# The first modulation units of a one-core decoder trunk: ten units of w_ada in five pairs, scale ahead of shift, and two input tiles from scaled activations with the shift added as a row

## The reference, cut to what matters

```python
c_act = jax.nn.silu(c)
mod = c_act @ ada_w[l] + ada_b[l]                 # (1024) @ (1024, 6144)
sh1, sc1, g1, sh2, sc2, g2 = jnp.split(mod, 6, axis=-1)
h = rms_norm(x, mix_norm[l]) * (1 + sc1) + sh1
xb, yb = jnp.split(h @ w_in, 2, axis=-1)          # (256, 1024) @ (1024, 2048)
# xb: causal conv of 4 taps, then r and i gates (8 blocks of 128x128), then a scan over the tokens
y = (hs * gelu(yb)) @ w_out
x = x + (1 + g1) * y
```

## Time and profile before

| | us |
|---|---|
| median of 3 runs | 1334.57 |
| lowest and highest | 1333.50, 1335.28 |
| span of the profiled execution | 1330.8 |
| the profiled execution's own whole-program time | not given |
| TensorE busy in the span | 1294.8 |
| VectorE busy | 577.2 |
| ScalarE busy | 267.4 |

### The profile page before, as it was taken

One profiled execution on the slowest core, in us unless ns is written; L12 is line 12 of the kernel. 1 busy time (PEld: TensorE's weight loads), 2 busy tenths in 40 slices (PEclk: granted clock), 3 DMA queues, 4 the chain that ended last, 5 costly groups with the idle time before them and its releaser, 6 DMA issues.

```text
span 1330.8 us, 27861 instructions
## 1 busy us (share of the span) xinstructions
PE 1294.8 (97%) x12266; PEld 810.1 (61%) x12267; DVE 577.2 (43%) x932; ACT 267.4 (20%) x496; POOL 13.0 (1%) x42
## 2 busy tenths in 40 slices
PE   7999899999998999999999999999999999999986
PEld 3888799999844763366345366456545355636622
DVE  2695998888766541232214033132122230422331
ACT  3572444444345540001001001000100000100000
POOL 1000000000000011000000000000000000000000
PEclk9999999999999999999999999999999999999999
DMA  9999758898954269999999999999999999999994
GB/s 353 353 385 338 239 203 310 319 316 312 388 214 162 90 254 399 380 357 418 418 418 418 419 419 419 418 418 418 418 418 418 418 418 419 418 419 418 419 418 198
DMA packets 129436, 477.62 MB, mean 359 GB/s; under 512 B 9408, under 2 KB 36256, under 8 KB 129312
## 3 DMA queue, kind: packets, MB, share of 16 engines
q1 hardware_dynamic: 129008, 475.23, 90.9%
q10 hardware_dynamic: 304, 0.57, 0.1%
HBM read 474.72 MB, written 1.05 MB: 357 GB/s over the span
## 4 chain that ended last, share of the span: by engine, by line
PE 90%; DMA 3%; SPq 3%; ACT 1%; DVE 1%; issue 1%; POOL 0%; ACTq 0%; POOLq 0%; DVEq 0%
PE psum L2077 36%; PE psum L2097 16%; PE psum L1816 5%; PE psum L1817 5%; PE psum L1818 5%; PE psum L1732 4%; SPq L667 3%; PE psum L1881 2%; PE psum L1938 2%; PE psum L1770 2%; PE psum L2055 2%; PE psum L2063 2%; DMA ring<-in_m_w_down 2%; DMA ring<-in_m_w_gu 2%; PE psum L1625 1%; PE psum L1632 1%
## 5 line engine op out<-in xcount | busy, mean ns | idle before, releaser
L2077 PE MATMUL psum<-ring,xe 128*32 128x448 f32 x4704 | 451.5, 539 | 1.4 <-DMA ring<-in_m_w_gu 1.4
L2077 PEld LDWEIGHTS psum<-ring,xe 128*32 128x32 f32 x4704 | 190.2, 110 | 252.0 <-issue 246.6
L2097 PE MATMUL psum<-ring,hT 128*32 128x256 f32 (+1 forms) x3180 | 247.6, 460 | 5.9 <-DMA ring<-in_m_w_down 5.7
L2097 PEld LDWEIGHTS psum<-ring,hT 128*32 128x32 f32 x3180 | 151.0, 110 | 95.8 <-issue 27.2
L1478 DVE TENSOR_TENSOR hs<-sg,psum 128x1344 f32<-128x1344 f32 x10 | 15.5, 1554 | 313.3 <-PE psum L2077 313.3
L1816 PE MATMUL psum<-fh,dhi 128*128 128x256 f32 x384 | 109.9, 286 | 3.7 <-DVE fl L1285 2.5
L1493 DVE STREAM_TRANSPOSE hT<-hs 32x448 f32<-32x448 f32 x120 | 111.8, 943 | 1.6
L1817 PE MATMUL psum<-fl,dhi 128*128 128x256 f32 x384 | 108.7, 283 | 0.0
L1818 PE MATMUL psum<-fh,dlo 128*128 128x256 f32 x384 | 108.6, 283 | 0.0
L864 ACT ACTIVATE dhi<-ring 128x1024 fp32r<-128x1024 f32 x72 | 75.9, 1060 | 90.9 <-PE psum L1818 86.1
L1251 DVE TENSOR_TENSOR dlo<-ring,dhi 128x1024 fp32r<-128x1024 f32 x72 | 88.2, 1225 | 6.9 <-ACT dhi L864 4.7
(11 more groups left out here) (298 smaller groups left out, 1196.3 us busy)
## 6 DMA issues: line engine op xcount, KB each, us to landing
ring<-in_m_w_gu SPq DMA_DIRECT2D x224, 896.0 KB, 23.2
ring<-in_m_w_down SPq DMA_DIRECT2D x118, 896.0 KB, 23.5
ring<-in_ada_w SPq DMA_DIRECT2D x24, 2048.0 KB, 16.1
ring_more<-in_m_w_gu SPq DMA_DIRECT2D x32, 896.0 KB, 22.6
ring<-in_f_w_gu SPq DMA_DIRECT2D x24, 1024.0 KB, 14.3
ring<-in_f_w_down SPq DMA_DIRECT2D x6, 2048.0 KB, 14.7
ring_more<-in_m_w_down SPq DMA_DIRECT2D x10, 896.0 KB, 24.5
ring<-in_a_w_in SPq DMA_DIRECT2D x4, 2048.0 KB, 19.5
```

What stands on the lines that cost most here:

```text
L2077: ins = mm(banks[TB * g:TB * g + TB, seg, 0:SEG], block(n), w[:, c0:c0 + SEG], start=first, stop=last, skip_group_check=True)
L2097: ins = mm(y_banks[TB * g:TB * g + TB, o0 + 256 * part:o0 + 256 * part + size], hT[:, t % 2, i, TB * b:TB * b + TB], raw(at // SW)[:, at % ...
```

## The change

The ten first units of w_ada become ten units of another cut: pair q holds units 2q and 2q+1, and its half h chunks 4h to 4h+3, so that a unit is 4 chunks of 128x1024 in pieces of 4 KB. Pair 1 (the scale) comes first, then w_in's first unit, then pair 0 (the shift). VectorE makes G = A * aff as soon as aff is there. TensorE makes tiles 0 and 1 of xb from G, and adds what the shift contributes: the shift, in a padded form (spad), times w_in's first unit gives a row, which a product with ones adds to every token. H is made by VectorE, and tiles 2 and 3 use it. VectorE's sums of units 4 to 9 become sums of pairs, 128x1024 per operation. gates(2) and gates(3) stand behind mix_in(3), ada(4) and ada(5) behind side_in(0). TensorE and ScalarE wait at the start for 7 constants, and TensorE for the rest behind the statistics. ScalarE's order behind the modulation (L827 on) is as before.

```diff
+        spad = dup[:, 32 * KC:64 * KC].rearrange("p (k m) -> p k m", k=KC)
+        pair_acc = lambda q: (sqb if q % 2 == 0 else qw)[:, :, :].rearrange("p b n -> p (b n)")
+        shift_row = rtmp[:, :]
...
+        ADA_ORDER = (2, 3, 0, 1)
...
+        def pair_unit(q, h):
+
+            src = ada_w[0].rearrange("(k p) n -> p k n", p=P)[:, 4 * h:4 * h + 4, 2 * UC * q:2 * UC * (q + 1)]
+            used = (row_mm, 2 * (1 - q) + h + 1) if q < 2 else (pair_half, pair_done(q) - 1 + h)
+            unit(("pair", q, h), [(lambda s: s[:, :].rearrange("p (k n) -> p k n", k=4), src)], used)
...
-        for v in range(4):
-            ada_unit(v)
+        pair_unit(1, 0)
+        pair_unit(1, 1)
         in_unit(0)
-        ada_unit(4)
+        pair_unit(0, 0)
+        pair_unit(0, 1)
         in_unit(1)
+        pair_unit(2, 0)
         unit("gates", [
...
-        ada_unit(5)
-        ada_unit(6)
+        pair_unit(2, 1)
         in_unit(2)
-        ada_unit(7)
-        ada_unit(8)
+        pair_unit(3, 0)
         in_unit(3)
-        ada_unit(9)
+        pair_unit(3, 1)
+        pair_unit(4, 0)
+        pair_unit(4, 1)
         out_unit(0)
...
+        CONSTS = 16 + SORTED
+        CONSTS_FIRST = 7
...
-            act.wait_ge(consts, CONSTS)
+            act.wait_ge(consts, CONSTS_FIRST)
...
             norm(0, [])
+            row_out(2)
+            row_out(3)
+            then(nc.scalar.activation(lru[:, 0, :], cols[:, CB_LAM:CB_LAM + 8], ACT.Abs), la)
+            then(nc.scalar.activation(lru[:, 1, :], lru[:, 0, :], ACT.Exp, scale=-1.0), la)
+            act.wait_ge(lam_d, 1)
+            then(nc.scalar.activation(lru[:, 3, :], lru[:, 2, :], ACT.Ln), la)
             row_out(0)
             row_out(1)
...
-            for k in range(KC):
-                act.wait_ge(xn_done, k // 2 + 1)
-                act.wait_ge(mod_ready, 1)
-                then(nc.scalar.activation(H[:, k, :], A[:, k, :], ACT.Identity, scale=aff[:, k:k + 1],
-                                          bias=mod[:, k:k + 1]), h_sig)
+            act.wait_ge(shift_mm_in, 1)
+            nc.scalar.activation(shift_row, bank[5][:, :], ACT.Copy).then_inc(shift_row_done, 1)
...
+            for v in (2, 3):
+                ada(v)
+            for k in range(KC):
+                v_.tensor_scalar(G[:, k, :], A[:, k, :], aff[:, k:k + 1], None, ALU.mult).then_inc(scaled_done, 1)
             dve.wait_ge(lam_a, 2)
             then(v_.tensor_scalar(lru[:, 2, :], lru[:, 1, :], 1.0, None, ALU.add), ld)
-            for v in range(ADA_ROWS):
+            for v in (0, 1):
                 ada(v)
+            v_.tensor_copy(spad[:, :, 0], mod[:, 0:KC]).then_inc(shift_ready, 1)
+            for k in range(KC):
+                v_.tensor_scalar(H[:, k, :], A[:, k, :], aff[:, k:k + 1], mod[:, k:k + 1],
+                                 ALU.mult, ALU.add).then_inc(shifted_done, 1)
...
-            ada_chunks(4)
+            pair_chunks(2, 0)
...
             for k in range(4):
                 conv(k)
-            ada(4)
-            ada_chunks(5)
-            for k in range(4, 6):
+            pair_chunks(2, 1)
+            for k in range(4, KC):
                 conv(k)
-            ada_chunks(6)
-            for k in range(6, KC):
-                conv(k)
-            ada(5)
...
+            ada(4)
+            ada(5)
+            pair_chunks(3, 0)
...
-            pe.wait_ge(consts, CONSTS)
+            pe.wait_ge(consts, CONSTS_FIRST)
...
+            def pair_as_rows(q, h):
+
+                w = arrived(("pair", q, h))[:, :].rearrange("p (k n) -> p k n", k=4)
+                for c in range(2):
+                    for k in range(4):
+                        last = mm(row_bank(c)[32 * k:32 * k + 32, :], cpad[:, 4 * h + k, :],
+                                  w[:, k, UC * c:UC * (c + 1)], start=h == 0, stop=h == 1)
                 last.then_inc(row_mm, 1)
...
             stats(0)
+            pe.wait_ge(consts, CONSTS)
             pe.wait_ge(cact_ready, 2)
+            pair_as_rows(1, 0)
             keep_clock(bank[5][:, :], 4)
+            pair_as_rows(1, 1)
             keep_clock(bank[5][:, :], 4)
             ada(2)
             ada(3)
             keep_clock(bank[5][:, :], 4)
...
+            def add_shift(T):
+
+                pe.wait_ge(shift_row_done, 1)
+                for a in range(2):
+                    i = 2 * T + a
+                    last = mm(side_bank(T)[:, SEQ * a:SEQ * a + SEQ], shift_row[:, i * P:(i + 1) * P],
+                              ones[:, None, :].to_broadcast([P, 2, P]), start=False, stop=a == 1, skip_group_check=True)
+                last.then_inc(xb_full, 1)
...
-            mix_in(0)
-            mix_in(1)
+            scaled_in(0)
+            pair_as_rows(0, 0)
+            scaled_in(1, [0])
+            pair_as_rows(0, 1)
+            scaled_in(1, [1])
+            ada(0)
+            ada(1)
+            keep_clock(bank[4][:, :], 4)
+            shift_as_row()
+            mix_in(2, [0])
+            add_shift(0)
+            add_shift(1)
+            mix_in(2, [1])
             for k in range(2):
                 gates(k)
-            ada(4)
-            mix_in(2)
-            for k in range(2, 4):
+            mix_in(3)
+            for k in range(2, 6):
                 gates(k)
-            mix_in(3)
-            for k in range(4, 6):
-                gates(k)
-            ada(5)
             side_in(0, [0])
             for k in range(6, KC):
                 gates(k)
             side_in(0, [1])
+            ada(4)
+            ada(5)
             side_in(1)
-            ada(6)
             side_in(2)
             side_in(3)
...
```

More of the change, by code:

```diff
@@ L263, in build @@
         lru_var = sem("lru_var")
+        pair_half = sem("pair_half")
+        scaled_done = sem("scaled_done")
+        shift_ready = sem("shift_ready")
+        shifted_done = sem("shifted_done")
+        shift_mm_in = sem("shift_mm_in")
+        shift_row_done = sem("shift_row_done")
         lru_beta = sem("lru_beta")
@@ L708, in _ @@
             do(nc.gpsimd.memset(cpad[:, :, :], 0.0))
+            do(nc.gpsimd.memset(spad[:, :, :], 0.0))
             do(nc.gpsimd.affine_select(out=ident[:, :], in_=ones[:, :], compare_op=ALU.is_equal, fill=0.0, base=0,
@@ L1123, in ada_chunk, with pair_chunks @@
                                                  op0=ALU.mult, op1=ALU.add), asum if k == KC - 1 else None)
+            def pair_chunks(q, h):
+                slot, at = full_at[name_of[("pair", q, h)]]
+                dve.wait_ge(ring_full[slot], at)
+                if h == 0:
+                    dve.wait_ge(ada_mm, max(2 * q - 2, ADA_ROWS))
+                for k in range(4 * h, 4 * h + 4):
+                    w = ring[slot][:, 2 * UC * (k % 4):2 * UC * (k % 4 + 1)]
+                    if k == 0:
+                        then(v_.tensor_scalar(pair_acc(q), w, cact[:, 0:1], None, ALU.mult))
+                    else:
+                        then(v_.scalar_tensor_tensor(out=pair_acc(q), in0=w, scalar=cact[:, k:k + 1], in1=pair_acc(q),
+                                                     op0=ALU.mult, op1=ALU.add), ph if k % 4 == 3 else None)
             def ada(v):
-                dve.wait_ge(ada_mm, v + 1)
+                dve.wait_ge(ada_mm, ada_place(v) + 1)
                 total = ada_bank(v)[:, 0:4]
@@ L1671, in stats @@
                     last.then_inc(stat_mm, 1)
[L1673 to L1678, removed]
+            def pair_as_rows(q, h):
[4 more added lines that the diff above has]
+                                  w[:, k, UC * c:UC * (c + 1)], start=h == 0, stop=h == 1)
                 last.then_inc(row_mm, 1)
             def ada(v):
-                if v >= 2:
-                    pe.wait_ge(ada_done, v - 1)
+                at = ada_place(v)
+                if at >= 2:
+                    pe.wait_ge(ada_done, at - 1)
                 if v < ADA_ROWS:
-                    pe.wait_ge(row_done, v + 1)
+                    pe.wait_ge(row_done, at + 1)
                 else:
-                    pe.wait_ge(ada_sum, ada_sum_at(v))
+                    pe.wait_ge(pair_half, pair_done(v // 2))
                 for i in range(UC // P):
@@ L1731, in in_products, with scaled_in, shift_as_row, mix_in @@
                 i = 2 * (T % 2) + a
[L1732 to L1740, removed]
-                    for k in range(KC):
-                        pe.wait_ge(h_done, k + 1)
-                        for a in range(2):
-                            last = in_products(T, k, a, start=k == 0 and a == 0, stop=k == KC - 1, skip_group_check=True)
-                last.then_inc(xb_full, 1)
+                return mm(side_bank(T % 4)[:, SEQ * a:SEQ * a + SEQ], w[:, k, i * P:(i + 1) * P],
+                          (G if T < 2 else H)[:, k, :], **how)
+            def scaled_in(T, halves=range(2)):
+                for k in range(KC):
+                    if T == 0:
+                        pe.wait_ge(scaled_done, k + 1)
+                    for a in halves:
```

(21 more changed lines are left out.)

48 lines of the change are left out of this document (15 added, 33 removed).

## The result

| us | before | changed |
|---|---|---|
| median of 4 runs each | 1334.92 | 1342.99 |
| lowest, highest | 1333.50, 1336.38 | 1341.09, 1347.73 |
| span of the profiled execution | 1330.8 | 1345.9 |
| its own whole-program time | not given | 1347.73 |
| dense stage starts | 142.25 | 150.51 |

The ratio is 1.0066, with an interval of 1.0045 to 1.0088: slower by 8.1 us, where 6.2 was forecast; 1342.99 lies within the range given. The profiled execution is the longest of the four, by 4.4 to 6.6 us.

The account below looks back on a forecast made before the run. It took TensorE's unbroken queue as the bound up to the dense stage. Front -1.3, gates 0 and 1 +0.9, gates 6 and 7 +7.1, start -1.3, clock +0.8 gave +6.2, 1340.8 us; range 1335.8 to 1344.3.

Parts of the forecast that it names:

- Gates 6 and 7: TensorE at gates(6) waits for ScalarE's chain from gates(2): 6.4 us, about 5 in one piece; gates(7) +0.7; together +7.1.
- Front: Statistics' end (T) to first input product: 11.2 us saved, 9.9 put behind the first product; together -1.3.
- Gates 0 and 1: TensorE waits 0.4 and 0.7 us for conv(0) and conv(1) behind VectorE's sums, 0.24 waited before: +0.9.
- Start: Waiting for 7 constants instead of 22 brings T earlier by at most 1.8 us; -1.3 taken.
- the possible 1.8: Most that T could come earlier at the start, bounded by unit two's landing at 17.8 to 18.3.
- Clock: Granted clock falls in the new 5 us gap ahead of gates(6): 0 to 1.6 us, +0.8 taken.
- the end of 0: Lower end of the clock term: the gap at gates(6) passes unpunished, costing 0.
- rival 1: Stall at gates(6) with the clock dropped in full, T not earlier: +8.3, 1342.9 us; chance 0.22.
- I count one for one: Later stages pass on any shift of the dense stage's start unchanged.
- The table load: ScalarE's two loads between gates: 1.28 us each; the skill's drain, 2.8 longer stall for two, not counted.

Follow-up runs that it names:

- e1: Changed kernel with ScalarE's first_tap(3) and gate_acts(4) to (7) directly behind gate_acts(3), all decays behind them: 1334.13 us, ratio 0.9989 against before.
- e3: Changed kernel with gates(2) and gates(3) ahead of mix_in(3) again on TensorE: 1336.32 us, ratio 1.0009 against before.
- e6: Kernel before with one move alone, gates(2) and gates(3) behind mix_in(3): 1342.38 us, ratio 1.0048 against before.
- e2: Changed kernel with 20 fillers in TensorE's gap ahead of gates(6): 1343.25 us, ratio 1.0051 against before.
- e5: Changed kernel with each pair unit loaded by two transfers in pieces of 2 KB: 1342.48 us, one run.
- e7: Changed kernel with e1's ScalarE order, gates in pairs between half tiles, second half of VectorE's pair 3 sum behind the scan: 1334.54 us, ratio 1.0002 against before.
- e9: e7 with 16 fillers instead of 5 at the start and 22 instead of 12 ahead of the dense stage: 1336.69 us, ratio 1.0005 against before.
- e10: e9 with 14 fillers at two attention waits, ada(8) and (9) behind the last round's second output product, VectorE's ada(8) later: 1331.33 us, ratio 0.9967 against before.
- e12: Changed kernel with all fillers (start, ahead of the dense stage, attention), its order untouched: 1341.46 us, ratio 1.0044 against before.
- e4: Changed kernel with TensorE and ScalarE waiting for all constants at the start again: 1342.88 us, one run.
- e8: Kernel before with e1's ScalarE order: 1335.34 us, ratio 1.0000 against before.
- e11: Kernel before with the fillers in attention and the 22 ahead of the dense stage: 1333.84 us, ratio 0.9984 against before.

## Why the prediction was right

**Gates 6 and 7, the main term: right in place, cause and size.** gates(6) started gates(2)+13.63, where the prediction had 13.4. Against the 6.93 of work between them it stood 6.70 (6.4 predicted), of which 4.95 in one piece ("about 5"). gates(7) followed 0.7 later than the work alone. That is 7.4 for 7.1. e1, e3 and e6 show the cause.

**Front: right in sum.** The first scaled product came at T+8.38 (T+8.4 predicted). From T to gates(0), with mix_in(2) added to before's side since it moved ahead, took 39.69 against 33.71+6.91: -0.9, where the prediction had -1.3. Gates 0 and 1 waited 0.69 (gates(1) alone), 0.5 more than before, for +0.9 predicted. Together -0.4, as predicted. The sums at 1285 ns and H at 407 ns were as taken; G, at 348 ns, was quicker than its 0.41.

**Start: mis-sized, and its 0.8 is a lucky draw.** "No row gives their landing", and most of the possible 1.8 was taken. The parameters landed late, at 8.5, so the first transpose came only 0.84 earlier (8.48 for 9.32). T followed it by 7.5 in both kernels and so moved by 0.8, not 1.3. The slow transposes of x, 3.49, cost nothing here: ScalarE's squares let the statistics start 3.8 to 3.9 behind the first transpose in both. In the other five profiled runs with this start (e1, e2, e3, e5, e7) the statistics products took 3.97 to 4.79 instead of 3.72, and T was 16.11 to 17.33. The mean of the six, 16.50, is 0.3 earlier than before's 16.77, and e5 is 0.6 later. The 16 fillers mend it: T is 15.51, 15.50 and 15.72 in e9, e10 and e12, and the statistics take 3.72 in all three.

**Clock: mis-sized, and one place missed.** The step took +0.8, the middle of 0 to 1.6. The records say 1.9: gates(6) and gates(7) took 0.3 and 0.85 more than their work and wait, and the half tile 4.23 instead of 3.47 to the next start, 0.76. e2 says 1.84 by another way. The same gap of 4.94 to 4.95 cost less elsewhere, by the same reading 1.0 in e4, 0.9 in e5 and 1.35 in e12, where the clock came back sooner. It never cost nothing; the end of 0 was no real one. The Trainium skill, "TensorE: Matmul & The Clock Gate", "HAM oscillation — how this bites in real kernels", which lets an array kept waiting start its next work cold, has this right for the gap at the gates.

**Sum at the dense stage:** T -0.8, front and gates 0 and 1 -0.4, gates 6 and 7 +7.4, clock +1.9: +8.1, and 8.26 was measured. The prediction's +6.2 lacks 0.5 at the start, 0.3 at the gates and 1.1 of clock. The measured 1342.99 is nearer to rival 1's 1342.9 than to the forecast's 1340.8: the same stall, the clock dropped in full, T not earlier. The first of these two conditions held, and with 0.3 in the mean the second nearly did.

**"I count one for one" failed by its clock.** The dense stage passed its start on with 1.5 us more, since the clock fell once more. The same stood in e1, e2, e4, e5 and e6 (229.8 to 229.9 from dense to K/V), not in before, e3, e7, e8, e9, e10, e11 and e12 (228.4). The median does not have all of it, as before's own runs from 1333.1 to 1341.2 may well have such falls.

**The table load.** Both switches in this stretch of the changed kernel read as the one of before does: 1.28 at 69.61 with the next activation at 70.90, and 1.28 at 76.04 with the next at 77.33. The Trainium skill, "ScalarE: Activation LUTs", "What ACT_TABLE_LOAD costs", adds a drain of 1.38 us to each. By it gates(6) would have come 2.8 later; it came 0.2 later than forecast (13.63 for 13.4), so the trace does not agree.

**What the change is worth without the loss.** e3 has T 0.7 and the front 0.9 earlier, yet its dense start is 1.24 later than before's. Four of its gates start 0.65 to 0.70 late, since conv and gate_acts come 1.55 us apart and a gate takes 0.86. What was won in the front is given back at the gates. Between e10 and e11, which share the fillers of the dense and attention stages, lie 2.5 us (the intervals of the ratios just overlap). This is the change together with a fitting order of three engines and a start without gaps; how it divides among these was not tried.

## What to carry to other kernels

When a piece of work moves in one engine's queue, lay the partner's queue beside it and take the distance from its feeder to the work that its result frees. Here ScalarE needed 13.4 us from gates(2) on, TensorE had 14.7 us of other work before the change and 7.0 after it. The price here was the wait and the half-rate work behind it. Filling the gap recovered the second part only (e2), reordering recovered both (e1, e3).

## What was not expected of the hardware

**The same short waits lower the clock in some executions and not in others.** The 2.47 us before the dense stage passed at 1.00 in the profiled run of before and fell to 0.52 in that of after. Two waits of 1.8 and 1.6 us in attention did the same, and so did the wait of 1.30 in e7. These falls are worth 1.5, 3.0 and 1.3 us. The first two would explain why the kernel before spreads over 6.8 us on one chip. With fillers at the dense start and in attention the highest of e11's 12 runs was 1336.37 and the highest of e10's 1332.92, while 11 of 30 runs of before on that chip lay above 1337. That the fillers narrow the spread is not shown by this: e12, which has them, spreads over 5.0 us in 7 runs, and e1, which has none of them, over 4.0 in 12 (1332.50 to 1336.47). What decides whether a wait is punished was not found.

**The granted clock can read 1.00 while the work is slow.** At the start the sixteen 128x128 transposes took 3.49 behind 3.45 us of idling (3.62 in five more runs with this start). Right behind five fillers they took 2.44 in before, and 2.19, 2.72 and 3.40 in e6, e8 and e11, whose code up to there is the same. They took 1.91 in e10, whose 16 fillers reach nearly up to them:

```profile
2.72 5.06 PE L1670 MATMUL psum<-ones,ident 128*128 128x512 bf16 x16 [2.72 <-POOL ident L736]
...
8.47 1.91 PE L1663 MATMUL psum<-ident,Dd 128*128 128x128 f32 x16
```

The window of after there:

```profile
10.00:12.00 2.00, 2.00 (x11) 2.00 (x10) 1.60 (x3) 1.94 (x4) 0.00 (x0) 1.00 1.03 416
```

The five fillers themselves take 2.31 there, where 4 take 0.97 later. So at the start of a run the column does not tell the rate, and durations of like products do. How long the slow rate lasts differs from run to run, with or without the idling.
